# Twelve units of modulation weights moved from TensorE to GpSimd, beside the projections and the attention

## What is computed

```python
for i in range(DEPTH):                      # DEPTH = 2, D = 1024
    sh1, sc1, g1, sh2, sc2, g2 = split(silu(c) @ w_mod[i] + b_mod[i], 6)   # w_mod[i]: 1024 x 6144
    h = x * (1 + sc1) + sh1
    mix = windowed_attention(h, hc) if i == 0 else short_conv(h)
    x = layer_norm(ALPHA * x + g1 * mix)
    h = x * (1 + sc2) + sh2
    ff = swiglu(h) if i == 0 else top2_of_8_experts(h)
    x = layer_norm(ALPHA * x + g2 * ff)
```

## Time and profile before

| | us |
|---|---|
| median of 3 runs | 2391.47 (2390.48 to 2394.78) |
| the profiled execution's own time | 2393.55 |
| its span in the trace | 2392.0 |

### The profile page before, as it was taken

The page is one execution under the profiler, slowest core; times in us unless marked ns, Lnnn a source line. Parts: engine busy times, 40 slices in busy tenths (PEclk is TensorE's granted clock), DMA queues, the critical chain, the costliest instruction groups (busy, mean ns, idle before and its releaser), DMA issues.

```text
span 2392.0 us, 29522 instructions
## 1 busy us (share of the span) xinstructions
PE 2247.4 (94%) x11176; PEld 1840.8 (77%) x11177; DVE 1473.9 (62%) x1310; ACT 1099.6 (46%) x1080; POOL 342.3 (14%) x211
## 2 busy tenths in 40 slices
PE   6989999999998999699999999999999999999990
PEld 4866678888877888587888888888787888888870
DVE  3456655435576445497544454459999994444976
ACT  4135534222224224576433343347777773343861
POOL 0000026888841000100000000000000000000004
PEclk8999989999998998799999999999999999999995
DMA  7420083555541212698555454559999996545953
GB/s 306 185 106 1 11 327 127 190 176 177 180 171 71 105 71 89 247 388 331 194 183 198 182 211 182 200 185 396 363 396 363 396 361 223 195 176 182 375 219 137
DMA packets 76174, 512.68 MB, mean 214 GB/s; under 512 B 8240, under 2 KB 8368, under 8 KB 19024
## 3 DMA queue, kind: packets, MB, share of 16 engines
q1 hardware_dynamic: 61344, 442.46, 48.6%
q0 software_dynamic: 14768, 69.35, 8.0%
HBM read 482.41 MB, written 29.36 MB: 214 GB/s over the span
## 4 chain that ended last, share of the span: by engine, by line
PE 90%; DVE 5%; DMA 2%; issue 1%; ACT 1%; POOL 0%; SPq 0%; POOLq 0%; DVEq 0%; ACTq 0%
PE ps L1602 26%; PE ps L1604 26%; PE ps L1603 26%; PE ps L552 2%; PE ps L507 2%; PE ps L563 2%; PE ps L1915 1%; DMA raw<-w_mod 1%; PE ps L1702 1%; PE ps L1651 1%; PE ps L511 1%; PE ps L1847 1%; DVE lo L1092 0%; PE ps L1708 0%; PE ps L1720 0%
## 5 line engine op out<-in xcount | busy, mean ns | idle before, releaser
L1602 PE MATMUL ps<-ah,hi 128*128 128x512 f32 x688 | 270.5, 393 | 8.2 <-DVE al L1218 6.5
L1603 PE MATMUL ps<-al,hi 128*128 128x512 f32 x688 | 269.2, 391 | 0.0
L1604 PE MATMUL ps<-ah,lo 128*128 128x512 f32 x688 | 269.0, 391 | 0.0
L1265 DVE TENSOR_TENSOR lob<-raw,hib 128x2048 fp32r<-128x2048 f32 x112 | 251.6, 2283 | 12.3 <-DMA dispatched_x<-ht,di 12.3
L1265 DVE TENSOR_TENSOR lo<-raw,hi 128x2048 fp32r<-128x2048 f32 x112 | 255.9, 2284 | 0.0
L1478 DVE TENSOR_TENSOR he<-se,ps 128x512 f32<-128x512 f32 x112 | 77.0, 687 | 290.1 <-ACT se L1000 289.7
L1265 DVE TENSOR_TENSOR loa<-raw,hia 128x2048 fp32r<-128x2048 f32 x112 | 251.1, 2283 | 1.1 <-ACT hia L870 1.1
L1602 PE MATMUL ps<-hia,xth 128*128 128x512 f32 x616 | 246.5, 400 | 4.9 <-issue 4.9
L1602 PE MATMUL ps<-hib,xth 128*128 128x512 f32 x616 | 245.5, 398 | 0.0
L1000 ACT ACTIVATE se<-ps 128x512 f32<-128x512 f32 x112 | 67.1, 599 | 387.4 <-PE ps L1604 387.4
L1602 PE MATMUL ps<-hi,hh 128*128 128x512 f32 x616 | 240.6, 391 | 2.2 <-DVE hl L1482 1.5
(11 more groups left out here) (250 smaller groups left out, 3929.3 us busy)
## 6 DMA issues: line engine op xcount, KB each, us to landing
raw<-w_moe SPq DMA_DIRECT2D x336, 1024.0 KB, 5.4
raw<-w_pre SPq DMA_DIRECT2D x59, 1024.0 KB, 5.0
raw<-w_mod POOLq DMA_DIRECT2D x28, 1024.0 KB, 5.1
raw<-w_mod SPq DMA_DIRECT2D x20, 1024.0 KB, 7.4
dispatched_x<-zt POOLq DMA_DIRECT2D x22, 512.0 KB, 9.5
xg<-dispatched_x POOLq DMA_DIRECT2D x8, 1024.0 KB, 6.9
expert_y<-ys POOLq DMA_DIRECT2D x8, 1024.0 KB, 5.1
expert_y<-zt POOLq DMA_DIRECT2D x6, 512.0 KB, 24.5
```

What stands on the lines that cost most here:

```text
L1265: dve.tensor_tensor(LO_OF[j], raw8(r), HI_OF[j].bitcast(F32), ALU.subtract).then_inc(raw_used[r], 1)
L1602: pe.matmul(outp, wh, ah, start=first, stop=False, skip_group_check=True)
L1603: pe.matmul(outp, wh, al, start=False, stop=False, skip_group_check=True)
L1604: return pe.matmul(outp, wl, ah, start=False, stop=last, skip_group_check=True)
```

## The change

- Units 8 to 19 are no longer loaded by SP nor multiplied on PE. POOL does them as it does units 20 to 47, in slot 3, as soon as the first eight vectors are formed (`mod_full` at 1) and slot 3 is free. The routine is now `mod_unit(u, part, total)`; its scratch is `MTE` (in the unused part of `HI[2]`), and its twelve results `ME[0..11]` lie in `LO[2]` and, from the ninth on, where `CXL` was, for which unit 8 waits for the second kv unit.
- PE loses the six `mod_pair` and `mod_cols`, ACT the six `mod_part`.
- Ahead of the output projection PE runs `mod_first`: it waits for the twelve sums and for the last attention output to leave bank 7 (`nt_ready`), then runs 24 matmuls of one column. DVE reads them after attention and not before it.
- SP loads the q units right behind the kv units, with nothing between them.
- POOL's loop over units 20 to 47 continues the counting; the load of unit 20 is issued during unit 19, ahead of the zeroing DMAs and not after the norm.

```diff
-            for e in range(MOD_E // 2):
-                load(2, w_mod[MOD_A + 2 * e])
-                load(3, w_mod[MOD_A + 2 * e + 1])
-                if e < 4:
-                    load(e % 2, w_pre[2 + e])
+            for u in range(2, 6):
+                load(u % 2, w_pre[u])
...
         @block.gpsimd
         def _(pool):
+            def mod_unit(u, part, total):
+                pool.wait_ge(modw_in, u * 16 + 16)
+                pool.tensor_tensor(w, w, silc, ALU.mult).then_inc(pool_step, 1)
+                pool.wait_ge(pool_step, u * 4 + 1)
+                pool.tensor_tensor(part[:], w[:, 0:4], w[:, 4:8], ALU.add).then_inc(pool_step, 1)
+                pool.wait_ge(pool_step, u * 4 + 2)
+                if u + 1 < n_units:
+                    fetch(u + 1)
+                pool.tensor_tensor(part[:, 0:2], part[:, 0:2], part[:, 2:4], ALU.add).then_inc(pool_step, 1)
+                pool.wait_ge(pool_step, u * 4 + 3)
+                pool.tensor_tensor(total, part[:, 0:1, :], part[:, 1:2, :], ALU.add).then_inc(pool_step, 1)
+                pool.wait_ge(pool_step, u * 4 + 4)
+                pool.sem_inc(mod_sums, 1)
+
+            pool.wait_ge(silc_ready, 1)
+            pool.wait_ge(raw_used[3], 1 + 2)
+            pool.wait_ge(mod_full, 1)
+            fetch(0)
+            for u in range(MOD_E):
+                if u == 8:
+                    pool.wait_ge(unit_done[1], 2)
+                mod_unit(u, MTE, ME[u][:])
+
             pool.wait_ge(ol_ready, 4 * NBLK)
...
-            pool.wait_ge(silc_ready, 1)
-            pool.wait_ge(raw_used[3], 1 + 2 + MOD_E // 2)
             pool.wait_ge(al_ready, 2 * KD)
-            fetch(0)
-            for u in range(n_units):
+            for u in range(MOD_B * N_MODB):
...
+                mod_unit(MOD_E + u, MT, MSB[:, slot:slot + 1, :])
...
-            def mod_part(e):
-                act.wait_ge(raw_used[3], 4 + e)
-                act.wait_ge(mod_full, 1)
-                act.activation(MP[e][:], PS[:, 6, :], ACT.Copy).then_inc(mrow_ready, 1)
...
                     cols_ = slice(2 * MOD_A, 2 * (MOD_A + MOD_E))
                     dve.wait_ge(mod_full, t.n("mod"))
-                    dve.tensor_tensor(MOD[:, 0, cols_], PS[:, 7, 0:2 * MOD_E], bmod[:, 0, cols_],
-                                      ALU.add).then_inc(mod_free, 1)
+                    dve.scalar_tensor_tensor(out=MOD[:, 0, cols_], in0=PS[:, 7, 0:2 * MOD_E], scalar=float(D),
+                                             in1=bmod[:, 0, cols_], op0=ALU.mult, op1=ALU.add).then_inc(mod_free, 1)
...
+            def mod_first():
+                pe.wait_ge(mod_sums, MOD_E)
+                pe.wait_ge(nt_ready, NPAIR // 2)
+                pe.wait_ge(mod_free, t.n("mod"))
+                for c in range(2 * MOD_E):
+                    ins = pe.matmul(PS[:, 7, c:c + 1], ME[c // 2][:, 0, (c % 2) * P:(c % 2 + 1) * P], mean_w[:, 0:1],
+                                    start=True, stop=True, skip_group_check=True)
+                ins.then_inc(mod_full, 1)
...
-                            mod_pair(2 + ns * i + j)
-                            mod_cols(1 + ns * i + j)
-                    mod_cols(MOD_E // 2 - 1)
...
                     if name == "o":
+                        mod_first()
                         pe.wait_ge(ol_ready, 4 * NBLK)
```

More of the change, by code:

```diff
@@ L231, in program @@
         MP = [put(f"mp{i}", [P, 512], F32, o_lo + 16384 + 2048 * i) for i in range(4)]
-        MP += [put(f"mp{i}", [P, 512], F32, o_hi + 18432 + 2048 * (i - 4)) for i in (4, 5)]
+        MTE = put("mte", [P, 4, 256], F32, o_hi + 18432)
+        ME = [put(f"me{i}", [P, 1, 256], F32, o_lo + 16384 + 1024 * i) for i in range(8)]
+        ME += [put(f"me{i}", [P, 1, 256], F32, r2 + 55296 + 1024 * (i - 8)) for i in range(8, MOD_E)]
         SILP = put("silp", [P, KD, 32], F32, o_hi + 16384)
@@ L687, in _, with fetch @@
         def _(pool):
+            silc = SILC[:, :, 0:1].to_broadcast([P, KD, 256])
+            w = RAW[3][:].rearrange("p (k n) -> p k n", k=KD)
+            n_units = MOD_E + MOD_B * N_MODB
+            def fetch(u):
+                pool.dma_start(RAW[3][:], w_mod[MOD_A + u]).then_inc(modw_in, 16)
+            def mod_unit(u, part, total):
[19 more added lines that the diff above has]
+                mod_unit(u, MTE, ME[u][:])
             pool.wait_ge(ol_ready, 4 * NBLK)
@@ L836, in _ @@
                 act.activation(XZ[:, k, :], XZ[:, k, :], ACT.Copy, scale=ALPHA).then_inc(alpha_done, 1)
-            for r in (2, 3):
-                t.skip(("raw", r), MOD_E // 2)
             act.wait_ge(mask_in, 16)
@@ L1670, in _ @@
             t.skip(("raw", 0), -1)
-            def mod_pair(e):
-                if e:
-                    pe.wait_ge(mrow_ready, MOD_A // 2 + e)
-                for j in range(2):
-                    mod_unit(2 + j, PS[:, 6, j * 256:(j + 1) * 256])
-            def mod_cols(e):
-                if e == 0:
-                    pe.wait_ge(mod_free, t.n("mod"))
-                pe.wait_ge(mrow_ready, MOD_A // 2 + e + 1)
-                for c in range(4):
-                    at = 4 * e + c
-                    ins = pe.matmul(PS[:, 7, at:at + 1], MP[e][:, c * P:(c + 1) * P], SEL[:, 0:1], start=True, stop=True,
-                                    skip_group_check=True)
-                if e == MOD_E // 2 - 1:
-                    ins.then_inc(mod_full, 1)
             def stats(stage):
@@ L1712, in _ @@
             fl_n = 0
+            def mod_first():
[6 more added lines that the diff above has]
+                ins.then_inc(mod_full, 1)
             def mod_batch(n):
-                pe.wait_ge(mod_sums, (n + 1) * MOD_B)
+                pe.wait_ge(mod_sums, MOD_E + (n + 1) * MOD_B)
                 pe.wait_ge(mod_free, t.n("mod"))
```

15 lines of the change are left out of this document (2 added, 13 removed).

## The result

The changed kernel takes 2415.82 us (median of 4 runs, 2410.58 to 2417.46), the kernel before beside it 2390.97 (2390.02 to 2394.78). The ratio is 1.0098, interval 1.0084 to 1.0113: slower by 24 us. The profiled execution took 2410.58, with a span of 2409.0. The stages tell where.

A forecast was written before the change was run, and what follows sets the result against it. The prediction took PE, which holds nearly all of the span and chain, to bound the kernel. Its seven terms sum to +23.4 us, which on 2391.47 gives 2414.9, predicted as 2415; range 2398 to 2438.

The forecast's parts named there:

- Part 1: First kv unit: POOL's arithmetic delays DVE's SBUF instructions, so the second kv unit starts 19.1 us later (bounds 8.0 to 23.5).
- The lock-step: First kv unit: POOL and DVE alternate, each POOL instruction holding one DVE SBUF instruction; some eight DVE instructions per 12.3 us.
- the second rival: POOL gets between DVE instructions less often, first kv unit costs 8 to 12.7; 2392 to 2405; chances 0.07 and 0.10.
- Part 2: Second kv unit: PE restarts at a reduced granted clock after idling, +1.5 us (0 to 3).
- Part 3: Behind the second kv unit and first three q units: PE loses four modulation pairs of 2.84 each, -11.4 us.
- Part 4: q units: POOL makes DVE's splits late and PE idles, +2 us for three such places (0 to 6).
- Part 5: End of q to attention: the split moves forward but exposed rotary instructions wait about 2.5, +0.2 us (-2.3 to +5).
- Part 6: Attention: three POOL units hold DVE's tiny instructions, 2.2 us a unit and a little, +7 us (0 to 14).
- Part 7: Ahead of the output projection: 24 one-column matmuls take 5.9 us, about 0.9 of it covered, +5.0 us.
- The rival in which PE is relieved and contention is hidden: DVE's instructions keep their times throughout, so the change is -8.7 us, giving 2382.8; chance 0.08.

The follow-up runs named there:

- e1: Changed kernel with POOL's arithmetic for units 8 to 19 left out, the loads kept and the results cleared; 2387.55 us, ratio 0.9984.
- e2: Changed kernel with one of the 24 one-column matmuls ahead of the output projection; 2522.62 us, a total that compares with nothing since the output differs.
- e5: The changed kernel run once more, with nothing altered; 2411.05 us, ratio 1.0086.
- e6: Changed kernel with the 24 columns spread among the output projection's first unit, three behind each of eight groups; 2419.63 us, ratio 1.0116.
- e9: Changed kernel with the 24 columns placed in attention, three in every second step from step 15 on; 2410.85 us, ratio 1.0075.
- e7: Kernel before with one SP load moved: the output projection's first unit, fetched ahead of the last pair of modulation units; 2388.51 us, ratio 0.9993.
- e3: Changed kernel with POOL's first load waiting until the second kv unit is done; 2411.88 us, ratio 1.0083.
- e4: Changed kernel with POOL's first load waiting for the last rotary tile, so all twelve units fall into attention; 2408.19 us, ratio 1.0073.
- e8: Changed kernel with POOL's four instructions a unit replaced by one-input multiplications by a constant, output wrong in value; 2399.19 us in one execution.
- e10: Changed kernel with POOL's two-input multiply of units 8 to 19 written as eight one-input multiplications of 256 elements; 2387.85 us, ratio 0.9995.

## Why the prediction was right in its total and wrong in its terms

Predicted were 2415.0 and slower, measured 2415.82. Mechanism and sign held. That the total fits to 1 us is luck: part 1 was up to 12 too dear, parts 4 to 7 up to 13 too cheap, and the errors cancelled. The second run of the same kernel gave 2411.05.

- **Part 1, +19.1 predicted, +7.4 to +14.1 measured.** This step failed. The lock-step is as drawn (3.72, 2.82, 1.93, 1.21), but it began 9.6 behind the load's issue and not 5.2 (at 44.3; drawn was 41.1, from an issue 1.2 later). The failing input is the load's 5.2: taken from a stretch in which only POOL loaded, where here SP's loads were still in flight. DVE used the time, and instead of three POOL units one fell on the chain in the changed kernel's profile, and one and a part of the second, or two, in the others. The lower bound of 8.0, one unit, was nearly the answer in the first. That is the size that the second rival gave this part, though not by its reasons: POOL did get in behind each DVE instruction, and L1144 was exposed. (The upper bound is 2.9 x 8.0 = 23.2 and not 23.5, and the lower end of that rival, +5, doesn't follow from its terms: 8 and the other 4.3 give +12.)
- **Part 2, +1.5 predicted.** No such loss shows: the second kv unit lasts 18.85, its 21.70 less the pair of 2.85.
- **Part 3, -11.4 predicted.** Held: in e1, where nothing else disturbs, the second kv unit and q are 2.9 and 9.0 shorter, 11.9 in all.
- **Part 4, +2 predicted, +5.9 to +6.6 measured** (50.12 and 49.44 of q against 43.55 in e1, nearly all of it). I had laid two units side by side, 0 and 1.4 late, and taken 2 for three such places. In the trace the two cycles locked: multiply and split start within 0.3 us of each other in three units running, 13.6 us apart on both engines, and each split takes 3.4 more. The three splits of 5.70 in a row stand in e2, e5, e6 and e9 as well.
- **Part 5, +0.2 predicted, +1.7 measured** in one profile and +0.1 in the other. The move of the split by 2.5 is confirmed by e7; the last split, caught again (131.12, 5.70), took it back.
- **Part 6, +7 predicted, +10.0 and +8.7 measured.** Four units fell into attention and not three, because it began at 144.8 (e5: 151.2) and not at 154; the ninth unit came at 146.8, drawn was 143. 1.6 of the loss is no contention, since e1 has it too. That leaves 8.4 and 7.1, 1.8 to 2.1 a unit on average, where 2.3 was the price; single units lie on both sides of it (e3, e4).
- **Part 7, +5.0 predicted, +9.3 measured.** The 5.9 were made from four matmuls at full clock. I left out the clock: 24 took 8.44, as the granted clock fell to 0.50 on the way, and the projection began at that level. The trace of before had the sign, in the norm's one-column matmuls at L1702, of which four (a row of x8) took 0.95 and 3 us later 1.84. e2 gives the sum, e9's stages show it nearly halved by a place in attention.
- **Behind o** I had written that a stage giving time back would speak against the prediction. Two do, by the clock: 1.5 at the norm that ends layer 0, and 2.2 at the second layer's first norm. So the 21.3 lost up to the output projection's statistics are 17.0 at the end of this execution.

Part 1 was 5 to 12 too dear; parts 4 to 7, 14.2 in the sum, came to 27.6 in the one profile and to 24.0 in the other, 10 to 13 too cheap.

The rival in which PE is relieved and contention is hidden (2383) was wrong for this kernel. With the contention taken away (e1) it would have been near: 2387.6, as the columns cost 7.7 there and not 5.0 and attention is 1.6 longer.

## What to carry to other kernels

Before moving work to GpSimd, list VectorE's SBUF instructions in that stretch that another engine waits for: each can be held for the length of one GpSimd instruction, and two cycles of similar length lock together. Then ask for another form of the GpSimd instruction: a multiply by one value per partition as several short one-input instructions took 2.7 times as long on GpSimd and left VectorE's instructions at nearly their own times. Time a load by what else is being loaded at that moment, and look at the granted clock wherever one-column matmuls are put: a block of them lowered it, and so did threes among projection matmuls, but not threes in attention.

## What the hardware did that I had not expected

- The granted clock fell from full to 0.50 during 8.44 us of nothing but one-column matmuls, though PE was never idle. Threes of them among projection matmuls kept it at 0.50 for 16 us (e6), and threes in every second attention step left it at 1.00 (e9). Why e6 and e9 differ is not settled.
- The first load on POOL's queue, 1 MB, took 7.9 to 9.6 us from its issue to its use in ten profiles, beside SP's loads, and 5.2 when it was alone (51.11 to 56.36 in the changed kernel).
- A one-input POOL instruction of 2048 elements held a DVE tensor_scalar for 5.2 us, to its own end, but two-input DVE instructions only until 3.5 us behind its start, for 2.0 at most (e8). Eight of 256 elements with a per-partition scalar held neither by more than 0.3 (e10). POOL's two-input adds still held DVE in e10.
- Two executions of one kernel differ by 6.7 us in the first kv unit alone, by which engine gets there first: with a contended engine one profile is not enough to size a term.
